# A two-stage transformer block with PEER on one Trainium2 core: the scattered gates are stored in 48 commands of 4 KB rows instead of 12 commands of 16 KB rows

## The chip, the cores and the metric

The kernel runs on 1 core of one Trainium2 chip. Times are device microseconds (us). The kernel before takes 1992.97 us, the median of 3 runs (1991.73 to 1994.1).

## What is computed

One pre-norm layer on 512 tokens of width 1024, all in float32: sliding-window attention and retention side by side, then PEER, then a per-layer embedding gate and a last norm. The change touches PEER alone. For every token and each of 8 heads, PEER takes 16 experts out of 128 x 128 by their scores, and sums them, weighted by a softmax over the 16:

```
top_s, top_pos = lax.top_k(cand, PEER_TOPK)
gates = jax.nn.softmax(top_s, axis=-1)
...
u = jnp.take(expert_down, idx, axis=0)
act = jax.nn.gelu(jnp.einsum('td,ted->te', hx, u, preferred_element_type=jnp.float32))
vv = jnp.take(expert_up, idx, axis=0)
return jnp.einsum('te,ted->td', (act * g).astype(hx.dtype), vv)
```

## The kernel before

**Weights.** All weights pass in 392 units of 128 x 1024 floats (512 KB). SP loads a unit into `raw` (4 slots), ACT rounds it to `w_hi` (L538, function `upper`), POOL subtracts to get `w_lo` (L488, function `lower`), and PE multiplies three times (L923 to L925: high by high, high by low, low by high). SP may load unit u when `lower` of unit u - 4 is done (`lo_done`); `w_hi` and `w_lo` are rings of 8.

**PEER in two ways.** For 384 tokens (12 groups of 32) it is dense: 128 units `dn` give the activations of all experts, 128 units `up` sum them up, and what multiplies the activations is a dense table of gates, zero where an expert was not taken. For the last 128 tokens it is sparse: POOL gathers rows of `peer_down` into 4 slots of `xT` (L512, 512 KB a gather), and DVE makes dot products of them (L1303, `dot`). The table `FETCH_AT` says behind which unit's `lower` POOL issues which gather. POOL works in order: a gather whose slot isn't free yet (`dot_done`) holds up every later `lower` and gather.

**The scatter stage.** Units 64 to 111 of `dn` are six turns (`gate_turn(j)`, j = 0 to 5) of 8 units (c = 0 to 7). In a unit PE makes, beside the 24 matmuls of the unit, two scatters (L1169), each of which spreads the gates of 4 tokens over 128 x 128 experts: one matrix of one-hot rows (DVE, L1659) times one that is multiplied by the gates (DVE L1667 or ACT L768). ACT copies the result from PSUM to `stage` (L755, `stage_gates`). `stage` has two halves, b = 0 and b = 1, each 128 partitions x 128 keys x 32 tokens, 2 MB, one for each half turn (4 units). When one is full, `store_gates` writes it to `gate_scratch` in DRAM (L761); the first copy into the same half, one turn later, waits for `gate_written[b]`. In a unit ACT does, in this order: a `stage_gates`, the products L768, `upper`, the gelu of the unit (L743), after every second one a store of activations to `act_scratch` (L746, 384 KB, rows of 3 KB), the second `stage_gates`, and, at c = 1 and c = 5, `store_gates`. PE may be two scatters ahead of `stage_gates` and two units ahead of the gelu.

**Behind the stage.** After the last turn ACT issues the last store, then makes the high part of `p` (L828), for which DVE waits (L1700) before it goes on with the dots that are left. 16 units of `dn` without scatters follow. The table is read back (L779) from the last eight units on, three key blocks ahead of its use in the `up` stage.

**Queues.** ACT's DMAs all go through one hardware queue (q10 in the profile), SP's through q1, POOL's gathers through q0. In the printed profile names, `stage` is a part of `scr`, so that the store reads `gate_scratch<-scr`.

Of the kernel before, what the change touches and what calls it, by code (L numbers as in the profile page):

```python
# [18 lines left out]
PH, NKEY, TOPK = 8, 128, 16  # L19
# [116 lines left out]
TG = 32  # L136
NTG = TD // TG
# [2 lines left out]
FIRST_Z = 7  # L140
EXP_AT, SELECT_AT = 4, 6
AHEAD = 2
RAW_Q = 4

NPAIR = PH * TOPK
# [31 lines left out]
def row_of(s):  # L177

    if NMAIN <= s < NMAIN + NX:
        return True, s - NMAIN  # L180
    return False, s if s < NMAIN else s - NX
# [15 lines left out]
def block_program(nc, xT_d, w_d, small_d, rope_r_d, decay_d, rope_a_d, mask_d, pT_d, down_d, up_d, out_d):  # L197
# [10 lines left out]
    gate_d = nc.dram_tensor("gate_scratch", (NTG, P, NKEY * TG), F32, kind="Internal").ap()  # L208
# [3 lines left out]
    with ExitStack() as ctx:  # L212
# [3 lines left out]
        def sem(name):  # L216
            return ctx.enter_context(nc.semaphore(name))
# [20 lines left out]
        def cut(at, n):  # L238
            assert at + n <= SCRATCH, (at, n)
            return scr[:, at:at + n]  # L240
# [55 lines left out]
        def v_slot(n):  # L296

            return v_ring[:, n % V_SLOTS, :]
# [9 lines left out]
        stage = cut(0, 8192).rearrange("p (b j t) -> p b j t", b=2, t=TG)  # L308
# [78 lines left out]
        gate_written = [sem("gate_written0"), sem("gate_written1")]  # L387
# [26 lines left out]
        w_rounds = w_d[0:NU // RAW * RAW].rearrange("(r s) p n -> s r p n", s=RAW)  # L414
        gate_quads = gate_d.rearrange("g p (i b n) -> b i p g n", b=2, n=JQ * TG)
        act_quads = act_d.rearrange("(i b a) p n -> b i p a n", b=2, a=2)
        gate_pairs = gate_d.rearrange("(i b) p n -> b i p n", b=2)
        act_pairs = act_d.rearrange("(i a) p n -> a i p n", a=STEP // 2)

        def scattered(q):  # L420
# [43 lines left out]
        @block.sync  # L464
        def _(sp):
            sp.dma_start(raw[:, 0, :], w_d[0]).then_inc(landed[0], 16)
            sp.dma_start(small[:, :], small_d).then_inc(small_landed, 16)
            for i in range(KT // 2):
                sp.dma_start(xT[:, 2 * i:2 * i + 2, :], xT_d[:, 2 * i:2 * i + 2, :]).then_inc(x_landed[i], 16)
            for s in range(1, RAW):  # L470
                sp.dma_start(raw[:, s, :], w_d[s]).then_inc(landed[s], 16)
            with sp.Fori(1, NU // RAW) as r:
                for s in range(RAW):
                    sp.wait_ge(lo_done, RAW * r + (s - RAW + 1))
                    sp.dma_start(raw[:, s, :], w_rounds[s][r]).then_inc(landed[s], 16)
            for u in range(NU // RAW * RAW, NU):
                sp.wait_ge(lo_done, u - RAW + 1)
                sp.dma_start(raw[:, u % RAW, :], w_d[u]).then_inc(landed[u % RAW], 16)
            for k in range(KT):
                sp.wait_ge(final_ready, k + 1)  # L480
                sp.dma_start(out_d[:, k, :], final[:, k, :]).then_inc(stored, 16)
            sp.wait_ge(stored, 16 * KT)


        @block.gpsimd
        def _(pool):
            def lower(s):
                return nc.gpsimd.tensor_tensor(w_lo[:, s, :], raw[:, s % RAW, :], w_hi[:, s, :].bitcast(F32),  # L488
                                               ALU.subtract)

            first = min(FETCH_DOWN) // RING
            with pool.Fori(0, first) as r:
                for s in range(RING):
                    pool.wait_ge(hi_done, RING * r + (s + 1))
                    lower(s).then_inc(lo_done, 1)
            for u in range(first * RING, NU):
                pool.wait_ge(hi_done, u + 1)
                lower(u % RING).then_inc(lo_done, 1)
                for r in FETCH_DOWN.get(u, ()):
                    extra, n = row_of(r)  # L500
                    if r == 0:
                        pool.wait_ge(x_spilled, 16)
                        pool.wait_ge(sq_ready, 2 * KT)
                        pool.wait_ge(h_ready, 3 * KT)
                    if extra:
                        pool.wait_ge(extra_ready, 1)
                    elif n % TOPK == 0:
                        pool.wait_ge(expert_ready, n // TOPK + 1)
                    if r >= U_SLOTS:
                        pool.wait_ge(dot_done, r - U_SLOTS + 1)  # L510
                    ids = expert_extra if extra else expert_of
                    pool.indirect_dma_start(u_ring[:, r % U_SLOTS, :], None, down_d,  # L512
                                            bass.IndirectOffsetOnAxis(ap=ids[:, n:n + 1], axis=0)
                                            ).then_inc(u_landed[r % U_SLOTS], 16)
                for n in FETCH_UP.get(u, ()):
                    if n == 0:
                        for b in range(2):
                            pool.wait_ge(gate_written[b], 16 * (NTG // 2))
                        pool.wait_ge(p_split, 2)
                    if n >= V_SLOTS:  # L520
                        pool.wait_ge(axpy_done, n - V_SLOTS + 1)
                    pool.indirect_dma_start(v_slot(n), None, up_d,  # L522
                                            bass.IndirectOffsetOnAxis(ap=expert_of[:, n:n + 1], axis=0)
                                            ).then_inc(v_landed[n % V_SLOTS], 16)
# [3 lines left out]
        def _(sc):  # L528
# [171 lines left out]
            def key_scores(m):  # L700
                sc.wait_ge(ks_done, m + 1)
                if m >= 8:
                    sc.wait_ge(s12_free, m - 7)
                nc.scalar.activation(s12[:, m % 8].rearrange("p t k -> p (t k)"), bank[:, 2 + m % 2, :],
                                     ACT.Copy).then_inc(s12_ready, 1)
# [3 lines left out]
            for k in range(KT):  # L709
                norm_upper(1, k)  # L710
                if k in (2, 6):
                    m = 1 + (k > 2)
                    run_ahead(UNIT[("pq", m)] + 4)
                    key_scores(m - 1)
            run_ahead(UNIT[("pq", RAW_Q - 1)] + 4)
            key_scores(RAW_Q - 2)
            sc.wait_ge(qp_ready, RAW_Q)
            for m in range(RAW_Q, 2 * PH):
                src = output(("pq", m))
# [29 lines left out]
            def stage_gates(j, q):  # L749

                b, t = q // (TG // 4), 4 * (q % (TG // 4))
                if t == 0 and j > 0:
                    sc.wait_ge(gate_written[b], 16 * j)
                sc.wait_ge(oh_used, 16 * j + (q + 1))
                nc.scalar.activation(stage[:, b, :, t:t + 4], scattered(q).rearrange("p t j -> p j t"),  # L755
                                     ACT.Copy).then_inc(stage_ready, 1)

            def store_gates(j, b):

                sc.wait_ge(stage_ready, 16 * j + 8 * (b + 1))  # L760
                sc.dma_start(gate_pairs[b][j], stage[:, b].rearrange("p j t -> p (j t)")).then_inc(gate_written[b], 16)  # L761

            def gate_odd(j, q):

# [19 lines left out]
            def gate_turn(j):  # L784
                for c in range(STEP):
                    stage_gates(j, 2 * c)
                    if 16 * j + 2 * c + 3 < TD // 4:
                        gate_odd(*divmod(16 * j + 2 * c + 3, 16))
                    gelu(j + (FIRST_Z + 1), c)
                    stage_gates(j, 2 * c + 1)  # L790
                    if c == 1 and j > 0:
                        store_gates(j - 1, 1)
                    if c == 5:
                        store_gates(j, 0)

            sc.wait_ge(filled, 1)
            gelu_turn(0)
# [19 lines left out]
            for j in range(NTG // 2):  # L817
# [3 lines left out]
                if j == TOK_AT[0]:  # L821
                    sc.wait_ge(extra_dotted, 1)
                    nc.scalar.activation(act_extra, turned, ACT.Gelu_apprx_tanh).then_inc(extra_gelu, 1)
            store_gates(NTG // 2 - 1, 1)
            sc.wait_ge(p_landed, 16)
            sc.wait_ge(oh_used, TD // 4)
            for k in range(2):
# [9 lines left out]
            def up_turn(i):  # L837
                last = i == NKEY // STEP - 1
                for c in range(STEP):
                    e = STEP * i + c  # L840
                    upper(UP0 + LEAD + e, (UP0 + LEAD + e) % RING)
                    if not last or c + AHEAD < STEP:
                        weight_upper(e + AHEAD, (c + AHEAD) % STEP)
                    if c % JQ == JQ - 1 and e // JQ + 3 < NKEY // JQ:
# [5 lines left out]
            for c in range(STEP):  # L850
                if c == STEP - 1:
                    for e in range(AHEAD):
                        weight_upper(e, e)
                gelu(NKEY // STEP - 1, c)
                if c == 0:
                    for b in range(2):
                        sc.wait_ge(gate_written[b], 16 * (NTG // 2))
                    read_back(0)
                if c == 3:
                    read_back(1)  # L860
# [59 lines left out]
        def _(pe):  # L920
# [205 lines left out]
            for m in range(2 * PH):  # L1126
                if m < RAW_Q:
                    columns(("pq", m), b_hi, b_lo, tiles=(u_ready, KT) if m == 0 else None,
                            at_tile={KT // 2: lambda: spread(1)} if m == 1 else {})
                else:  # L1130
                    columns(("pq", m), h_hi, h_lo, tiles=(h_ready, 2 * KT) if m == RAW_Q else None)
                if m == RAW_Q:
# [735 lines left out]
```

## Time and profile before

| what | value |
|---|---|
| median of 3 runs | 1992.97 us |
| profiled execution, its own time | 1998.92 us |
| profiled execution, span of the records | 1997.1 us |
| PE busy | 1961.2 us (98%) |
| DVE, POOL, ACT busy | 1313.9, 1226.6, 803.8 us |
| gate stores (L761) | 12 of 2048 KB, median 12.7 us from issue to landing |
| gathers of `peer_down` (L512) | 160 of 512 KB, median 7.0 us |
| weight loads | 390 of 512 KB, median 5.4 us |

The profiled execution took 5.95 us more than the median of the others. The scatter stage lies at about 1060 to 1334 us of the span, the `up` stage at about 1400 to 1900 us. The ends of PE's matmuls are modelled, so its busy time may hold a little of its waiting too.

### The profile page before, as it was taken

To read this page: it belongs to the slowest core of one execution; us is meant where nothing else is said; L and a number is where in the kernel's file an instruction comes from. 1 tells how busy PE (TensorE), PEld (TensorE's weight loads), DVE (VectorE), ACT (ScalarE), POOL (GpSimd) and SP (SyncE) were. 2 spreads that over 40 slices of the span, in tenths; PEclk is the share of its full clock that TensorE was granted. 3 is DMA by queue.
4 is the path that set the end of the run, shared out by engine and by line. 5 is a ranking of instruction groups with operands and counts; after the bars stand their busy time and mean duration, and the time that the engine had idled before them with its cause. 6 is when DMAs were issued, how large, how long until landed. Compare 5 with 4: busy or idle time off the path is not lost.

```text
span 1997.1 us, 28913 instructions
## 1 busy us (share of the span) xinstructions
PE 1961.2 (98%) x10211; PEld 1725.5 (86%) x10211; DVE 1313.9 (66%) x2287; ACT 803.8 (40%) x1273; POOL 1226.6 (61%) x682
## 2 busy tenths in 40 slices
PE   7999999999999999999999999999999999999997
PEld 6888888888888888999999999999888888888886
DVE  6433333333732389988967888861897898888846
ACT  6222222233553333443345666663343333333352
POOL 5342424243234333898877666667899888888821
PEclk9999999999999999999999999999999999999998
DMA  6232313242223332999987999999999999999921
GB/s 210 74 112 62 115 59 107 72 137 80 80 85 95 103 118 79 332 339 329 353 307 258 392 362 365 372 384 315 350 380 387 370 363 355 366 362 363 357 64 43
DMA packets 171953, 471.93 MB, mean 236 GB/s; under 512 B 13776, under 2 KB 62928, under 8 KB 170064
## 3 DMA queue, kind: packets, MB, share of 16 engines
q1 hardware_dynamic: 58032, 209.04, 30.9%
q0 software_dynamic: 41472, 151.01, 19.9%
q10 hardware_dynamic: 72352, 110.64, 15.8%
q8 instruction: 54, 0.88, 0.2%
q14 instruction: 43, 0.35, 0.1%
HBM read 413.49 MB, written 54.53 MB: 234 GB/s over the span
## 4 chain that ended last, share of the span: by engine, by line
PE 69%; DMA 10%; DVE 9%; POOL 8%; issue 2%; ACT 1%; DVEq 0%; SPq 0%; ACTq 0%; POOLq 0%
PE bank L923 22%; PE bank L925 21%; PE bank L924 21%; DMA xT<-peer_down,scr 9%; POOL w_lo L488 6%; POOL xT L512 3%; DVE xT L1303 3%; PE bank L1031 1%; PE bank L1114 1%; DMA gate_scratch<-scr 1%; PE bank L1099 1%; DVE b_hi L1659 1%; DMA raw<-weights 1%; PE bank L1075 0%; PE bank L1085 0%
## 5 line engine op out<-in xcount | busy, mean ns | idle before, releaser
L488 POOL TENSOR_TENSOR w_lo<-raw,w_hi 128x1024 fp32r<-128x1024 f32 x390 | 936.9, 2411 | 570.1 <-ACT w_hi L538 566.0
L923 PE MATMUL bank<-h_hi,w_hi 128*128 128x352 f32 (+2 forms) x1560 | 550.9, 353 | 9.7 <-ACT scr L743 8.9
L925 PE MATMUL bank<-h_hi,w_lo 128*128 128x352 f32 (+2 forms) x1560 | 539.2, 346 | 0.0
L924 PE MATMUL bank<-h_lo,w_hi 128*128 128x352 f32 (+2 forms) x1560 | 538.2, 345 | 0.0
L538 ACT ACTIVATE w_hi<-raw 128x1024 fp32r<-128x1024 f32 x390 | 405.9, 1053 | 283.1 <-DMA raw<-weights 139.4
L923 PEld LDWEIGHTS bank<-h_hi,w_hi 128*128 128x128 f32 x1560 | 294.4, 189 | 31.9 <-POOL w_lo L488 7.3
L924 PEld LDWEIGHTS bank<-h_lo,w_hi 128*128 128x128 f32 x1560 | 295.3, 189 | 19.8
L925 PEld LDWEIGHTS bank<-h_hi,w_lo 128*128 128x128 f32 x1560 | 293.7, 188 | 20.9
L923 PE MATMUL bank<-w_hi,b_hi 128*128 128x512 f32 x768 | 298.8, 389 | 0.0
L925 PE MATMUL bank<-w_hi,b_lo 128*128 128x512 f32 x768 | 298.8, 389 | 0.0
L924 PE MATMUL bank<-w_lo,b_hi 128*128 128x512 f32 x768 | 298.8, 389 | 0.0
L1303 DVE SCALAR_TENSOR_TENSOR xT<-xT,bank 128x1024 f32<-128x1024 f32 x160 | 193.5, 1212 | 78.4 <-DMA xT<-peer_down,scr 74.0
L1732 DVE TENSOR_TENSOR b_lo<-scr,b_hi 128x384 fp32r<-128x384 f32 x128 | 186.6, 1458 | 82.2 <-ACT b_hi L835 81.9
L512 POOL DMA_INDIRECT xT<-peer_down,scr x160 | 151.7, 948 | 122.2 <-DVE xT L1303 88.7
L923 PEld LDWEIGHTS bank<-w_hi,b_hi 128*128 128x128 f32 x768 | 144.1, 188 | 30.0
L925 PEld LDWEIGHTS bank<-w_hi,b_lo 128*128 128x128 f32 x768 | 144.1, 188 | 29.9
L924 PEld LDWEIGHTS bank<-w_lo,b_hi 128*128 128x128 f32 x768 | 144.1, 188 | 29.8
L522 POOL DMA_INDIRECT scr<-peer_up,scr x128 | 137.9, 1077 | 49.0 <-DVE bank L1712 29.0
L835 ACT ACTIVATE b_hi<-scr 128x384 fp32r<-128x384 f32 x128 | 67.2, 525 | 244.0 <-PE bank L925 145.0
L1712 DVE SCALAR_TENSOR_TENSOR bank<-scr,bank 128x1024 f32<-128x1024 f32 x127 | 162.2, 1277 | 0.8
L923 PE MATMUL bank<-b_hi,w_hi 128*128 128x512 f32 x272 | 108.1, 398 | 10.5 <-DVE b_lo L1318 9.1
L923 PE MATMUL bank<-w_hi,h_hi 128*128 128x512 f32 (+1 forms) x288 | 109.7, 381 | 1.1 <-DVE h_lo L1351 1.1
(215 smaller groups left out, 2446.9 us busy)
## 6 DMA issues: line engine op xcount, KB each, us to landing
raw<-weights SPq DMA_DIRECT2D x390, 512.0 KB, 5.4
act_scratch<-scr ACTq DMA_DIRECT2D x64, 384.0 KB, 5.8
gate_scratch<-scr ACTq DMA_DIRECT2D x12, 2048.0 KB, 12.7
scr<-gate_scratch ACTq DMA_DIRECT2D x22, 768.0 KB, 9.9
scr<-act_scratch ACTq DMA_DIRECT2D x22, 768.0 KB, 15.4
xT<-gate_scratch ACTq DMA_DIRECT2D x10, 768.0 KB, 9.1
xT<-act_scratch ACTq DMA_DIRECT2D x10, 768.0 KB, 13.8
scr<-scr ACTq DMA_DIRECT2D x20, 128.0 KB, 2.9
```

Source lines behind the costliest of these rows:

```text
L488: return nc.gpsimd.tensor_tensor(w_lo[:, s, :], raw[:, s % RAW, :], w_hi[:, s, :].bitcast(F32), ALU.subtract)
L512: pool.indirect_dma_start(u_ring[:, r % U_SLOTS, :], None, down_d, bass.IndirectOffsetOnAxis(ap=ids[:, n:n + 1], axis=0)).then_inc(u_lande ...
L522: pool.indirect_dma_start(v_slot(n), None, up_d, bass.IndirectOffsetOnAxis(ap=expert_of[:, n:n + 1], axis=0)).then_inc(v_landed[n % V_SLOT ...
L538: nc.scalar.activation(w_hi[:, u_mod, :], raw[:, s, :], ACT.Copy).then_inc(hi_done, 1)
L835: nc.scalar.activation(b_hi[:, c % 4, 0:TD], wgt[:, c % 2, :], ACT.Copy).then_inc(wgt_hi_ready, 1)
L923: nc.tensor.matmul(out, a_hi, c_hi, start=first, stop=False)
L924: nc.tensor.matmul(out, a_hi, c_lo, start=False, stop=False)
L925: return nc.tensor.matmul(out, a_lo, c_hi, start=False, stop=last)
L1031: ins = nc.tensor.matmul(bank[:, 2 + j, 0:S - P * j], r_k[:, c, P * j:P * j + P], r_q[:, c, P * j:S], start=c == 0, stop=c == 1)
L1303: stt(out=row, in0=row, scalar=1.0, in1=h_tok, op0=ALU.mult, op1=ALU.mult, accum_out=to[:, n:n + 1]).then_inc(dot_done, 1)
L1712: ins = stt(out=y_sparse, in0=v_slot(n), scalar=a, in1=y_sparse, op0=ALU.mult, op1=ALU.add)
L1732: tt(b_lo[:, c % 4, 0:TD], wgt[:, c % 2, :], b_hi[:, c % 4, 0:TD].bitcast(F32), ALU.subtract).then_inc(wgt_split, 1)
```

## The change

A half of `stage` is written by four commands instead of one, each for 32 of the 128 keys: 128 partitions x 1024 floats, 4 KB in a row at both ends, 512 KB a command. Two are issued one unit earlier than the one command was, behind c = 4 (or c = 0), and two where it was, behind c = 5 (or c = 1). The last half has its four commands together. The waits count 4 x 16 for a half. The bytes and their places in DRAM stay, and so does everything that reads them.

```
+GATE_PARTS = 4
...
-        gate_pairs = gate_d.rearrange("(i b) p n -> b i p n", b=2)
+        gate_parts = gate_d.rearrange("(i b) p (j t) -> b i p j t", b=2, t=TG)
...
                 if t == 0 and j > 0:
-                    sc.wait_ge(gate_written[b], 16 * j)
+                    sc.wait_ge(gate_written[b], 16 * GATE_PARTS * j)
...
-            def store_gates(j, b):
+            def store_gates(j, b, parts):
 
                 sc.wait_ge(stage_ready, 16 * j + 8 * (b + 1))
-                sc.dma_start(gate_pairs[b][j], stage[:, b].rearrange("p j t -> p (j t)")).then_inc(gate_written[b], 16)
+                for x in parts:
+                    part = slice(x * NKEY // GATE_PARTS, (x + 1) * NKEY // GATE_PARTS)
+                    sc.dma_start(gate_parts[b][j][:, part], stage[:, b, part, :]).then_inc(gate_written[b], 16)
...
-                    if c == 1 and j > 0:
-                        store_gates(j - 1, 1)
-                    if c == 5:
-                        store_gates(j, 0)
+                    if c in (0, 1) and j > 0:
+                        store_gates(j - 1, 1, (2 * c, 2 * c + 1))
+                    if c in (4, 5):
+                        store_gates(j, 0, (2 * c - 8, 2 * c - 7))
...
-            store_gates(NTG // 2 - 1, 1)
+            store_gates(NTG // 2 - 1, 1, range(GATE_PARTS))
```

ACT's instructions at units c = 4 and c = 5 of the first turn, where the first half is stored; `scr<-bank` of L755 are the copies into `stage`. Before:

```order
L755 ACTIVATE scr<-bank 128x128x4 x2
L768 ACTIVATE scr<-b_hi,scr 128x128 x4
L538 ACTIVATE w_hi<-raw 128x1024
L743 ACTIVATE scr<-bank 128x352
L746 DMA act_scratch<-scr 128x768
L755 ACTIVATE scr<-bank 128x128x4
L761 DMA gate_scratch<-scr 128x4096
L755 ACTIVATE scr<-bank 128x128x4
```

The same place of the changed kernel (its lines stand one to three lower):

```order
L756 ACTIVATE scr<-bank 128x128x4
L764 DMA gate_scratch<-scr 128x1024 x2
L756 ACTIVATE scr<-bank 128x128x4
L771 ACTIVATE scr<-b_hi,scr 128x128 x4
L539 ACTIVATE w_hi<-raw 128x1024
L744 ACTIVATE scr<-bank 128x352
L747 DMA act_scratch<-scr 128x768
L756 ACTIVATE scr<-bank 128x128x4
L764 DMA gate_scratch<-scr 128x1024 x2
```

The first two parts now stand ahead of a store of activations in ACT's queue, the other two behind it. ACT behind the last turn, before:

```order
L746 DMA act_scratch<-scr 128x768
L755 ACTIVATE scr<-bank 128x128x4
L761 DMA gate_scratch<-scr 128x4096
L828 ACTIVATE b_hi<-scr 128x512 x2
L538 ACTIVATE w_hi<-raw 128x1024
```

and in the changed kernel:

```order
L747 DMA act_scratch<-scr 128x768
L756 ACTIVATE scr<-bank 128x128x4
L764 DMA gate_scratch<-scr 128x1024 x4
L831 ACTIVATE b_hi<-scr 128x512 x2
L539 ACTIVATE w_hi<-raw 128x1024
```

Four commands now stand ahead of the high part of `p` where there was one.

## Rows read from the trace of the kernel before

**Rows 1.** Busy time by stretch: stretch, length, engines (us, count), PEclk, DMA share, GB/s.

```profile
1058.30:1061.70 3.40, 3.40 (x15) 3.40 (x15) 1.93 (x4) 1.52 (x5) 3.22 (x3) 0.50 0.79 235
1069.50:1336.50 267.00, 266.57 (x1897) 265.63 (x1896) 214.18 (x284) 169.58 (x371) 184.40 (x121) 1.00 0.94 357
1336.50:1372.00 35.50, 33.09 (x205) 32.54 (x204) 11.88 (x20) 12.79 (x18) 25.83 (x14) 1.00 0.91 332
1400.00:1900.00 500.00, 500.00 (x2207) 414.01 (x2207) 430.34 (x376) 188.93 (x249) 439.87 (x254) 1.00 1.00 365
```

**Rows 2.** PE in order of time: start, duration, instruction, [idle before <- releaser].

```profile
1057.39 0.40 PE L923 MATMUL bank<-h_hi,w_hi 128*128 128x352 f32 x1 [3.54 <-ACT scr L743]
...
1158.95 1.16 PE L1169 MATMUL bank<-scr,b_lo 128*128 128x128 f32 x8 [0.37 <-DVE scr L1667]
...
1353.94 0.43 PE L923 MATMUL bank<-h_hi,w_hi 128*128 128x352 f32 x1 [0.52 <-POOL w_lo L488]
...
1359.96 0.40 PE L923 MATMUL bank<-h_hi,w_hi 128*128 128x352 f32 x1 [1.89 <-ACT scr L743]
```

**Rows 3.** The chain of waits ahead of PE's last two restarts: start, us, what.

```profile
1329.87 19.14 DMA xT<-peer_down,scr
...
1349.03 1.24 DVE xT L1303 x2
...
1351.48 2.40 POOL w_lo L488
...
1357.59 2.23 DMA raw<-weights
```

**Rows 4.** DVE in order of time, ahead of the restart at 1158.95.

```profile
1155.94 1.22 DVE L1303 SCALAR_TENSOR_TENSOR xT<-xT,bank 128x1024 f32<-128x1024 f32 x1 [4.43 <-DMA xT<-peer_down,scr]
```

**Rows 5.** DMA queues from 1341 to 1346: packets, MB, share of 16 engines.

```profile
DMA packets 203, 2.15 MB, mean 429 GB/s; under 512 B 21, under 2 KB 21, under 8 KB 89
...
q10 hardware_dynamic: 119, 1.87, 87.4%
q0 software_dynamic: 79, 0.26, 12.8%
```

**Rows 6.** DMA queues from 1337 to 1340.

```profile
DMA packets 341, 1.22 MB, mean 406 GB/s; under 512 B 18, under 2 KB 18, under 8 KB 341
...
q1 hardware_dynamic: 119, 0.48, 40.8%
q0 software_dynamic: 119, 0.42, 36.1%
q10 hardware_dynamic: 103, 0.31, 25.8%
```

**Rows 7.** DMA queues from 1346 to 1351: the gathers'.

```profile
q0 software_dynamic: 275, 1.01, 49.4%
```

**Rows 8.** ACT in order of time: two gelus, two gate stores.

```profile
1100.23 0.45 ACT L743 ACTIVATE scr<-bank 128x352 f32<-128x352 f32 x1
...
1105.86 0.44 ACT L743 ACTIVATE scr<-bank 128x352 f32<-128x352 f32 x1
...
1324.99 0.71 ACTq L761 DMA_DIRECT2D gate_scratch<-scr  x1
...
1334.89 0.33 ACTq L761 DMA_DIRECT2D gate_scratch<-scr  x1
```

**Rows 9.** Who waited for whom, 1066 to 1330: us in total, times, longest.

```profile
ACT scr L755 <- PE bank L1169: 44.2, 31, 3.9
...
ACT scr L755 <- DMA gate_scratch<-scr: 10.4, 4, 3.7
```

**Rows 10.** DVE and POOL behind the last gate store.

```profile
1342.93 1.22 DVE L1303 SCALAR_TENSOR_TENSOR xT<-xT,bank 128x1024 f32<-128x1024 f32 x1 [3.05 <-DMA xT<-peer_down,scr]
...
1339.30 0.95 POOL L512 DMA_INDIRECT xT<-peer_down,scr  x1 [6.09 <-DVE xT L1303]
```

**Rows 11.** The gathers of `peer_down` (L512) issued from 1095 to 1335.

```profile
DMA to landing us min/median/max: 4.3/11.0/19.1
```

More of the change, by code:

```diff
@@ L517, in _ @@
                         for b in range(2):
-                            pool.wait_ge(gate_written[b], 16 * (NTG // 2))
+                            pool.wait_ge(gate_written[b], 16 * GATE_PARTS * (NTG // 2))
                         pool.wait_ge(p_split, 2)
@@ L856, in _ @@
                     for b in range(2):
-                        sc.wait_ge(gate_written[b], 16 * (NTG // 2))
+                        sc.wait_ge(gate_written[b], 16 * GATE_PARTS * (NTG // 2))
                     read_back(0)
```

## The prediction, made before the changed kernel ran

> **What bounds the kernel now.** The page shows PE busy for 98% of the span, so a store in another engine's queue can only matter where PE waits. Where that is, the stretches say [rows 1]. From the first gate store to the end of the scatter stage (1069.5 to 1336.5) PE is busy for 266.57 of 267.00 us; in the 35.5 us behind it for 33.09. So all that PE loses where a gate store is in flight is 0.43 + 2.41 = 2.84 us. Ahead of 1069.5 the change does nothing, and the `up` stage (1400 to 1900) has PE at 500.00 of 500.00 us although its DMA share is 1.00.
>
> PE in order of time shows the same loss as three restarts [rows 2]: idle for 0.37 us at 1158.95, 0.52 at 1353.94 and 1.89 at 1359.96, together 2.78 us.
>
> What do they hang on? The chain of waits answers for the last two [rows 3]: a gather of `peer_down` issued at 1329.87 lands after 19.14 us, the dot at 1349.03 waits for it, POOL's next gather waits for the dot's slot, `lower` at 1351.48 stands behind that gather, and PE waits for this `lower` at 1353.94. The weights that came late through all this land last (1357.59), and make the wait of 1.89 us. The restart at 1158.95 waits for DVE's L1667, which stands behind a dot that waited 4.43 us for its gather [rows 4]. So all three hang on gathers that land late, none on ACT's own wait for a gate store. Those waits are there (4, together 10.4 us, the longest 3.7) but ACT has cover for them: it waits 44.2 us for PE in the same stretch [rows 9].
>
> Why do the gathers land late? The DMA queues from 1341 to 1346 [rows 5]: 203 packets, of which only 89 are under 8 KB; the other 114 are the 16 KB rows of the last gate store. Its queue has 87.4% of the engines and the gathers 12.8%, though a gather is pending all the time. Four us earlier, where q10 still moves activations in rows of 3 KB, the three queues have 40.8, 36.1 and 25.8% [rows 6]. **A queue gets its turn by packets, not by bytes: rows of 16 KB push the others aside, rows of 3 or 4 KB share.**
>
> **The change part by part.**
>
> *Rows of 4 KB instead of 16 KB.* This is the part with a gain. In the 5 us of [rows 5] the gathers moved 0.26 MB. With the share of [rows 6] it is 0.42 MB in 3 us, so 0.70 MB in 5 us: 0.44 MB more by 1346. Behind that the gathers ran at 1.01 MB in 5 us, 0.20 MB per us [rows 7], so the late one lands 0.44 / 0.20 = 2.2 us earlier. The whole chain of [rows 3] hangs on it and moves by 2.2 us. To do away with both restarts it would have to move by 0.52 + 1.89 = 2.41 us. Gain 2.2, and 0.2 stays. The restart at 1158.95 is 0.37 us behind a wait of 4.43 for a gather, and goes: gain 0.4. Bounds: nothing (the gather is late for another reason) to 2.84 (every stall goes).
>
> *Four commands instead of one.* 36 commands more on ACT. A command took 0.33 to 0.71 us [rows 8]. In a scatter turn they are two more at c = 0 and c = 4, at most 1.4 us in a unit's 5.63 us (the distance of two gelus, the same rows), and one more at c = 1 and c = 5, at most 0.7. ACT waits for PE 31 times, 44.2 us in all [rows 9], 1.4 us each, just behind the `stage_gates` where the commands now stand. Price 0; with that cover gone, 1.4 us per half turn.
>
> The Trainium skill, "DMA: Bandwidth & Descriptors", section "Rules for kernel authors", speaks against this part: at least 1 MiB per DMA. Its section "Anatomy of one DMA" has, for the path through GpSimd, a fit of 2.0 us fixed plus the bytes at 436 GB/s for each. By that, as an estimate, four commands of 512 KB would need 6 us more than one of 2 MB if nothing overlapped. The trace doesn't bear it out for queued commands: the weights and gathers of [rows 6] are commands of 512 KB, and the engines moved 406 GB/s beside 429 for the large rows of [rows 5].
>
> That ratio is the price in engine time: 2 MB take 5.2 us of all engines instead of 4.9, 0.3 us for each of 12 halves, 3 us in a stretch with a DMA share of 0.94 over 267 us, so 16 us free [rows 1]. Hidden.
>
> *Half of it a unit earlier.* The store now shares, so it takes longer, and it has 16.9 us (three units of 5.63) from its first command to the copy that needs the half, instead of 11.3. Suppose q10 has only the even share all the time: 2.1 MB at 0.16 MB per us (0.48 MB in 3 us for rows of 4 KB, [rows 6]) are 13.1 us, 0.39 MB of activations between them at 0.10 are 3.8, and I allow 2 for a command's start (the last store, issued at 1334.89, ran from about 1341 on behind activations). That is 18.9 us, 2.0 more than there is. ACT then waits 2 us per half, in the range of what it now waits (up to 3.7) without a restart of PE. With the others idle at times the share is higher and there is no wait. Price 0.
>
> *The last half, four commands ahead of L828.* Three more commands delay `p`'s high part by 3 x 0.33 = 1.0 to 3 x 0.71 = 2.1 us. Behind it: DVE's L1700, the dots, and POOL, which waited 6.09 us for a dot [rows 10]. The dot at 1342.93 waits 3.05 us for its gather anyway, which takes up the delay on DVE; the gathers POOL issues at 1339.30 are later by as much, and are used only behind 1350. Price 0; bounds 0 and 2.1.
>
> **Sum.** 2.2 + 0.4 = 2.6 us off. On the profiled execution 1998.92 becomes 1996.3; on the median, 1992.97 becomes **1990.4 us**. The medians lie 5.95 us under the profiled time; what the profiler adds is not known, and if it adds DMA work, the unprofiled runs may have less of these stalls to lose.
>
> 0.2% is 4.0 us, about what a measurement of this kernel can tell from no change. So even the whole 2.84 us would count as no change.
>
> **Rivals.**
>
> *The gathers don't profit (chance 0.20).* Sharing may go by commands, or the last gather may be late for what stands ahead of it in its own queue (19.14 us is more than the 5 us of one gate store). For it: two gate stores, of 1324.99 and 1334.89, fall into its flight, and one command can hold only part of that. Against it: the even shares of [rows 6] with rows of 3 and 4 KB. Then 1992 to 1994, no change.
>
> *More than 4.0 us (0.11).* The stalls that show are worth 2.84. PE's busy time is modelled and may hold waits of a few hundredths at many of the scatters; for 94 half units in 267 us, 0.015 us each would be 1.4, together 4.2 us: 1988.8. Faster.
>
> *ACT becomes late (0.07).* The other side. The place is the first copy into a half of `stage`. From the first command it has 16.9 us and some 3.7 us of wait that PE didn't feel, 20.6 us. If q10 gets less than its even share, say 0.12 MB per us, a half takes 2.1 / 0.12 + 3.8 + 2 = 23.3 us, and PE waits 2.7 us in each of ten half turns (the first and the last have no successor): 1992.97 + 27 - 0.4, about 2020 us. It decides from a landing of the second pair some 15 us behind its issue.
>
> *The end gets worse (0.05).* The 2.1 us of the last four commands go through to PE, nothing is won, and the wait of 1.89 us becomes 4.0. A wait of 3.54 us at 1057.39 [rows 2] was followed by 3.4 us in which the granted clock was 0.50, 1.2 GHz [rows 1], 1.7 us lost. Together 3.8 to 4.5 us: 1997.
>
> **How the numbers follow.** The forecast has 0.57, the rivals 0.20, 0.11, 0.07 and 0.05. Faster 0.11, same 0.77, slower 0.12. The range: down to 1992.97 - 2.84 - 1.2 (the spread of the runs shown) - 0.5 (a third of the hidden waits) = 1988.4, with some 0.08 of the fast case under it; up to 1992.97 + 2.5 = 1995.5, where the rival without a gain pays the upper bound of 2.1 for the last four commands, with the two slow cases over it.
>
> **What would show it.** Right: queue q10 has at most half of the engines while gates are stored; the median landing of L512 from 1095 to 1335 falls under its 11.0 us [rows 11]; the three restarts are gone or one of under 1 us is left behind 1350; ACT's wait for `gate_scratch` is no longer than 4 us; PE busy for over 34.5 of the 35.5 us behind the stage. Wrong: gathers still at 11 us or more with rows of 4 KB in q10 (sharing is not by packet), or PE idle in the scatter stage with ACT L755 behind `gate_scratch` (the store is too slow).

## The result, and the profile after

The changed kernel takes 1998.43 us, median of 20 runs (1993.44 to 2007.28), beside 1991.93 us for the kernel before (20 runs, 1987.88 to 1995.4): a ratio of 1.0029, 95% interval 1.002 to 1.0037. It is slower, by 5.8 us by this ratio and by 6.5 us from median to median, where 2.6 us less was forecast, and outside the range. (Of the weights, the section on the kernel speaks of 392 units; the profile's loads are 390.)

The profiled execution of the changed kernel took 1995.74 us, 3.2 us less than the profiled one before. That pair misleads: 1998.92 us was more than every one of the 20 runs before, and 1995.74 is the sixth fastest of the 20 after.

Stretches of the changed kernel, as [rows 1]:

```profile
1069.50:1336.50 267.00, 267.00 (x1902) 267.00 (x1901) 214.95 (x282) 168.28 (x372) 183.09 (x120) 1.00 0.97 369
1336.50:1372.00 35.50, 32.22 (x202) 31.95 (x201) 10.89 (x19) 12.96 (x19) 28.98 (x16) 1.00 0.85 280
```

PE is never idle in the scatter stage, but loses 3.28 us behind it, where it lost 2.41. Who waited for whom there, from 1066 to 1330, as [rows 9]:

```profile
POOL xT L513 <- DVE xT L1306: 44.3, 30, 3.4
...
ACT scr L756 <- DMA gate_scratch<-scr: 13.5, 4, 4.9
...
DVE xT L1306 <- DMA xT<-peer_down,scr: 5.2, 4, 2.9
```

The gathers do land earlier, issued from 1095 to 1335, as [rows 11]:

```profile
DMA to landing us min/median/max: 4.9/8.1/12.1
```

So the half of the prediction that spoke of the gathers came true: the median fell from 11.0 to 8.1 us, DVE's wait for them from 34.7 (20.8 in the second trace of the kernel before) to 5.2 us, and the restart at 1158.95 is gone. What came instead stands behind the last turn. ACT in order of time (ACTq marks the commands that ACT issues):

```profile
1330.46 0.60 ACT L756 ACTIVATE scr<-bank 128x512 f32<-128x512 f32 x1 [0.43 <-PE bank L1172]
1331.09 3.24 ACTq L764 DMA_DIRECT2D gate_scratch<-scr  x4
1334.44 1.16 ACT L831 ACTIVATE b_hi<-scr 128x512 fp32r<-128x512 f32 x2 [3.37 <-issue]
```

DVE and POOL at the same place, as [rows 10]:

```profile
1335.17 1.42 DVE L1703 TENSOR_TENSOR b_lo<-scr,b_hi 128x512 fp32r<-128x512 f32 x2 [11.86 <-ACT b_hi L831]
...
1338.41 0.95 POOL L513 DMA_INDIRECT xT<-peer_down,scr  x1 [11.22 <-DVE xT L1306]
```

The chain of waits from there to PE, in order of time, as [rows 3]:

```profile
1331.09 0.33 ACTq L764
1331.45 0.54 ACTq L764
1332.01 1.05 ACTq L764
1333.10 1.24 ACTq L764
1334.44 0.64 ACT b_hi L831
...
1336.62 1.24 DVE xT L1306 x2
...
1348.95 2.42 POOL w_lo L489
1351.53 4.85 DMA raw<-weights
```

and PE's restart at its end:

```profile
1356.75 0.40 PE L926 MATMUL bank<-h_hi,w_hi 128*128 128x352 f32 x1 [3.29 <-ACT scr L744]
```

**The four commands of the last half hold ACT for 3.24 us, each longer than the one ahead of it.** The high part of `p` waits behind them, DVE waits for `p` with its last dots behind that, POOL waits for the dots with its gathers and `lower`s, and these free the slots of the weights.

The second trace of the kernel before (below), in which PE loses nothing here, shows the same three places:

```profile
1329.72 0.33 ACTq L761 DMA_DIRECT2D gate_scratch<-scr  x1
...
1330.89 1.42 DVE L1700 TENSOR_TENSOR b_lo<-scr,b_hi 128x512 fp32r<-128x512 f32 x2 [8.95 <-ACT b_hi L828]
...
1334.13 0.95 POOL L512 DMA_INDIRECT xT<-peer_down,scr  x1 [8.31 <-DVE xT L1303]
```

The store holds ACT for 0.33 us there and for 3.24 us in the changed kernel, 2.91 us more. DVE's wait for `p` is longer by 2.91 us too, and POOL's wait for the dots by 2.91 us. PE loses 3.28 us at the end of this chain.

In 9 of the 20 runs the mean granted clock was 0.996 or more, with a mean time of 1996.0 us; in 11 it was 0.995 or less, with a mean of 2000.5.

### The profile page after: what moved, and what is told of

The parts are those of the page before. It is cut to its first block, busy times and chain, and to the rows that moved or that the text cites. A ratio compares the mean times of both kernels' runs of the same rounds, so it can differ in the third digit from the quotient of the medians.

```text
span 1993.9 us, 28949 instructions
## 1 busy us (share of the span) xinstructions
PE 1957.6 (98%) x10211; PEld 1724.2 (86%) x10211; DVE 1310.4 (66%) x2287; ACT 802.3 (40%) x1273; POOL 1227.2 (62%) x682
## 4 chain that ended last, share of the span: by engine, by line
PE 81%; POOL 7%; DVE 6%; DMA 3%; ACT 1%; issue 1%; ACTq 0%; DVEq 0%; SPq 0%; POOLq 0%
PE bank L926 24%; PE bank L928 24%; PE bank L927 24%; POOL w_lo L489 5%; PE bank L1172 4%; POOL xT L513 2%; DMA xT<-peer_down,scr 2%; DVE xT L1306 1%; PE bank L1034 1%; DMA raw<-weights 1%; PE bank L1117 1%; PE bank L1102 1%; PE bank L1078 0%; PE bank L1088 0%; DVE scr L1597 0%
```

## The experiments

Two theories. **E, the end**: the loss is the hold of ACT ahead of `p`, behind the last turn. **S, the stage**: the store, sharing the engines, comes late for the copies into `stage`, half turn for half turn.

### The changed kernel again; `p` first; the last half in one command

Four kernels: the changed one again (`a_again`); the changed one with the high part of `p` ahead of the last store (`a_pfirst`); the kernel before with the same move (`b_pfirst`); the changed one with its last half stored in one command, as before (`a_lastone`).

```
# a_pfirst, b_pfirst: moved ahead of the last store_gates
sc.wait_ge(p_landed, 16)
sc.wait_ge(oh_used, TD // 4)
for k in range(2):
    nc.scalar.activation(b_hi[:, 6 + k, :], pT[:, k, :], ACT.Copy).then_inc(p_hi_ready, 1)
# a_lastone: the last half
sc.dma_start(gate_last, stage[:, 1].rearrange("p j t -> p (j t)")).then_inc(gate_written[1], 16)
```

Changed kernel again. 

> The changed kernel once more, as the measure for its neighbours on the same chip. Theory E (the end): its loss comes from behind the last scatter turn, where four commands hold ACT for about 3 us ahead of the high part of p, and PE idles 3 to 4 us near 1353; the time is then 4 to 7 us over the kernel before, and the trace shows no stall of PE from 1095 to 1335. Theory S (the stage): the loss is made of waits of the copies into the stage for their store, and the trace shows PE stalls there.

`p` first, changed kernel. 

> The changed kernel with the high part of p ahead of the last half's four commands instead of behind them. Theory E: the delay of DVE behind the last turn shrinks by some 3 us, PE's stall near 1353 by 3 us, and the time falls by 3 to 6 us against the changed kernel, to the kernel before or under it. Theory S: no change against the changed kernel, 5 to 6 us over the kernel before.

`p` first, kernel before. 

> The kernel before with the same move. Its one command took 0.33 us there. Theory E: at most 0.5 us less than before, so no difference. If it gains more than 2 us, what matters is not ACT's time for the command but that p is ready earlier for another reason.

Last half in one command. 

> The changed kernel with the last half stored by one command of 2 MB in rows of 16 KB, as before; the other eleven halves stay in four commands each. Theory E: the time falls to that of the kernel before (within 2 us), since ACT is held for 0.3 instead of 3.2 us. Theory S: no change against the changed kernel. If the last store's rows of 16 KB push the gathers and weights aside (the prediction's mechanism), this one is slower than the variant with p ahead by 1 to 2 us.

| kernel | median us (runs) | ratio to before, 95% |
|---|---|---|
| before, same chip | 1993.34 (35) | |
| changed, again | 1998.05 (12) | 1.0025 (1.0012 to 1.0038) |
| changed, `p` first | 1991.8 (12) | 0.9994 (0.9981 to 1.0006) |
| before, `p` first | 1992.1 (12) | 0.9996 (0.998 to 1.0011) |
| changed, last half in one | 1991.68 (12) | 0.9994 (0.9981 to 1.0008) |

Each of the two, `p` first and the last half in one command, takes the whole loss of the changed kernel away, 6.3 and 6.4 us from median to median, with 11 halves still in four commands and their rows of 4 KB. So E holds, and S falls. On the kernel before, `p` first makes no difference that can be told, as expected. That the rows of 16 KB of the last store cost 1 to 2 us more than four commands behind `p` does not show.

The second trace of the changed kernel has what the first lacked. Its four commands:

```profile
1332.36 3.27 ACTq L764 DMA_DIRECT2D gate_scratch<-scr  x4
```

PE's restart, two matmuls behind it and two some microseconds later:

```profile
1358.77 0.63 PE L926 MATMUL bank<-h_hi,w_hi 128*128 128x352 f32 x1 [4.04 <-ACT scr L744]
...
1363.60 0.49 PE L927 MATMUL bank<-h_lo,w_hi 128*128 128x352 f32 x1
1363.90 0.49 PE L928 MATMUL bank<-h_hi,w_lo 128*128 128x352 f32 x1
...
1364.65 0.32 PE L928 MATMUL bank<-h_hi,w_lo 128*128 128x352 f32 x1
1364.81 0.33 PE L926 MATMUL bank<-h_hi,w_hi 128*128 128x352 f32 x1
```

The stretches there:

```profile
1357.70:1364.40 6.70, 5.63 (x19) 5.66 (x20) 1.13 (x2) 3.29 (x5) 6.05 (x3) 0.50 0.86 264
...
1336.50:1372.00 35.50, 31.46 (x180) 31.20 (x180) 12.13 (x20) 12.71 (x18) 26.61 (x15) 0.90 0.79 261
```

The granted clock is 0.50 (1.2 GHz) for 6.7 us, from the last 1.07 us of an idle time of 4.04 us on. The 18 matmuls from 1358.77 to 1364.19 take 5.4 us, about 0.29 us from start to start; at the 0.16 us of the rows behind them they would take 2.9. So the clock costs some 2.5 us on top of the wait. The span is 2000.0 us, as against 1993.9 in the first trace, where 3.29 us of idle were followed by no such stretch. Of the 6.1 us, 2.5 are the clock and 0.75 the longer wait; 1.3 lie ahead of the last store (1332.36 as against 1331.09), and PE loses 1.1 us in the `up` stage (498.91 busy of 500.00). With `p` first:

```profile
1336.50:1372.00 35.50, 35.50 (x224) 35.50 (x223) 6.06 (x10) 14.11 (x20) 30.30 (x15) 1.00 0.95 316
```

PE has no idle time left here and the clock stays at 1.00; the span is 1988.6 us. ACT is held no less than before, but now with `p` ahead of it:

```profile
1329.26 0.86 ACTq L764 DMA_DIRECT2D gate_scratch<-scr  x2
...
1330.14 2.63 ACTq L764 DMA_DIRECT2D gate_scratch<-scr  x2
...
1333.09 0.95 POOL L513 DMA_INDIRECT xT<-peer_down,scr  x1 [7.72 <-DVE xT L1306]
```

`upper` and the gelus stand behind these commands as well, and nothing is lost.

### The end alone; the dots first; one command with small rows; the kernel before again

```
# b_lastfour: kernel before, the last half alone (gate_last = gate_d[NTG - 1]; the waits count 48 more)
for x in range(4):
    sc.dma_start(gate_last[:, 1024 * x:1024 * x + 1024],
                 stage[:, 1, 32 * x:32 * x + 32].rearrange("p j t -> p (j t)")).then_inc(gate_written[1], 16)
# a_dotsfirst: changed kernel, on DVE
next_dots(NLAST)                      # was behind the split of p
ve.wait_ge(oh_used, TD // 4)
for k in range(2):
    ve.wait_ge(p_hi_ready, k + 1)
    ...
# b_rows4k: DRAM laid out (NTG, P, 4, 1024 + 128), one command per half
sc.dma_start(gate_rows[b][j], stage[:, b].rearrange("p (x j) t -> p x (j t)", x=4))
```

The end alone. 

> The kernel before with the last half alone in four commands of 4 KB rows; the other eleven halves as before. Theory E (four commands back to back hold ACT for some 3.2 us ahead of the high part of p): the whole loss is here, 4 to 7 us over the kernel before, PE idle for 3 to 4.5 us near 1353, and in some runs a stretch at 1.2 GHz behind it. Rival (the end only hurts because the earlier gathers of the changed kernel bring DVE to its wait for p sooner): under 2 us over the kernel before.

Dots first. 

> The changed kernel with the last dots of DVE ahead of its wait for p instead of behind it; ACT keeps its order. Theory E says that the late p costs only because the dots, and with them POOL's gathers and lower parts, stand behind it on DVE: the time falls by 4 to 7 us against the changed kernel, POOL's wait of 11 us behind the last turn goes, and PE has no stall near 1353. Rival (ACT's delay of 3 us itself reaches PE, through the weights' high part or the gelu): no change against the changed kernel.

Rows of 4 KB in one command. 

> The kernel before with its one command per half, at its place, but in rows of 4 KB (four parts of a row lie 512 B apart in DRAM): the size of the rows alone. By the prediction's mechanism the gathers land in 8 to 9 us instead of 11 in the scatter stage, and PE has no stall there; the time is that of the kernel before less 0 to 3 us, and ACT issues the command in under 1 us. If rows of 4 KB cost ACT as much as four commands do, the issue of the last one takes about 3 us and the time is 4 to 7 us over the kernel before.

The kernel before again. 

> The kernel before once more, for a second trace. Its first trace took 1998.9 us, more than any unprofiled run near it. If the stalls of PE behind the last turn (2.4 us in the first trace) are typical, they are here again; if they were bad luck, PE is never idle from 1095 to 1900 and the span is near 1990 us, so that the changed kernel had nothing to win.

| kernel | median us (runs) | ratio to before, 95% |
|---|---|---|
| before, same chip | 1991.55 (19) | |
| before, last half in four | 1995.98 (10) | 1.0023 (1.0012 to 1.0033) |
| changed, dots first | 1990.55 (10) | 0.9997 (0.9986 to 1.0009) |
| before, one command, rows of 4 KB | 2013.62 (4) | 1.0116 (1.0094 to 1.0137) |
| before, again | 1992.35 (1) | |

Splitting **the last half alone** costs 4.4 us from median to median, where the changed kernel lost 6.5 and, in its repetition, 4.7. The intervals of the ratios overlap, so no rest is shown. PE restarts at 1354.63:

```profile
1354.63 0.40 PE L927 MATMUL bank<-h_hi,w_hi 128*128 128x352 f32 x1 [3.57 <-ACT scr L744]
```

followed by 3.2 us at a granted clock of 0.50:

```profile
1356.10:1359.30 3.20, 3.20 (x13) 3.20 (x12) 0.00 (x0) 1.33 (x2) 3.20 (x3) 0.50 0.76 247
```

With **the dots first**, ACT is still held,

```profile
1332.05 2.09 ACTq L764 DMA_DIRECT2D gate_scratch<-scr  x4
```

yet PE's busy time behind the stage is full and the loss is gone:

```profile
1336.50:1372.00 35.50, 35.50 (x224) 35.50 (x223) 7.55 (x12) 14.52 (x20) 24.87 (x12) 1.00 0.89 317
```

So ACT's hold reaches PE through DVE, where the dots stand behind `p`, and not through ACT's own work. The hold is also shorter here, 2.09 us; why, these runs don't tell, and by itself this trace would leave open that the shorter hold made the difference. `p` first doesn't: there ACT was held for 2.63 us by the last two commands alone.

**The kernel before**, in its second trace:

```profile
1069.50:1336.50 267.00, 267.00 (x1900) 267.00 (x1899) 217.88 (x288) 169.56 (x370) 184.07 (x123) 1.00 0.96 367
1336.50:1372.00 35.50, 35.50 (x224) 35.50 (x223) 6.64 (x12) 14.05 (x20) 31.27 (x15) 1.00 0.92 326
```

None of the 2.84 us of [rows 1] is there, so in this execution the change had nothing to win. Of the 6.5 us between the two spans (1997.1 and 1990.6), 5.2 lie ahead of the last gate store (issued at 1334.89 and at 1329.72). The expectation failed in one point: PE does lose 1.17 us in the `up` stage (498.83 busy of 500.00).

**Rows of 4 KB in one command** cost 22 us, where a gain of 0 to 3 was expected. The gathers do land somewhat earlier (a median of 8.9 us over 1095 to 1336.5, as against 9.3 in the second trace of the kernel before), but the other side of sharing decides: the store lands late. Landings of the gate stores, and the waits from 1095 to 1336.5:

```profile
DMA to landing us min/median/max: 13.9/16.9/20.5
```

```profile
ACT scr L758 <- DMA gate_scratch<-scr: 57.9, 10, 8.8
...
PE bank L1172 <- ACT scr L758: 11.0, 5, 3.1
```

The median landing of the store was 12.7 us in the first trace before and 11.5 in the second. Now it is late for 10 half turns and PE idles for 11.0 us; what makes up the rest of the 22 I did not part. ACT issues the command in 0.52 us, so small rows by themselves don't hold ACT.

### All four at the old place; four commands of 16 KB rows; both moves

```
# a_notearly: all four where the one was
if c == 1 and j > 0:
    store_gates(j - 1, 1, range(GATE_PARTS))
if c == 5:
    store_gates(j, 0, range(GATE_PARTS))
# b_cmds4: kernel before, four commands of 32 partitions, rows of 16 KB
for x in range(4):
    at = slice(32 * x, 32 * x + 32)
    sc.dma_start(gate_pairs[b][j][at], stage[at, b].rearrange("p j t -> p (j t)")).then_inc(gate_written[b], 16)
```

None early. 

> The changed kernel with all four commands of a half where the one command was, none a unit earlier. The one command with 4 KB rows at that place landed after 16.9 us, over the 11.3 us that are left, ACT waited 57.9 us and PE was late by 11 us in the stage, 22 us in all. If the share of q10 makes that (rows of 4 KB share, whoever issues them), this kernel too is 15 to 30 us slower than before, with PE waiting for the copies into the stage. If it was the single command or its padded rows in DRAM, this one is at the changed kernel, 4 to 7 us over before.

Four commands, large rows. 

> The kernel before with every half in four commands of 32 partitions each, rows of 16 KB, at the place of the one: the count of commands alone. Theory E: ACT is held for about 3 us ahead of the high part of p, and the loss is that of the last four commands alone, 3 to 6 us; in the stage no stall of PE. If the rows' size makes ACT's hold, there is none here (0.33 us a command) and the time is that of before. If four commands per half hold ACT inside the stage too, over 8 us.

Both moves (`p` first and dots first), changed kernel. 

> The changed kernel with both mends, the high part of p ahead of the last store and the last dots ahead of the wait for p. Each alone took away the stall near 1353, so together they should give no more: within 2 us of either, 0 to 3 us under the kernel before, not to be told from it. If the earlier gathers of the 4 KB rows are worth something once the end is mended, it shows here as more than 2 us under the same two moves on the kernel before.

Both moves, kernel before. 

> The kernel before with the same two moves. PE had no stall from 1095 to 1900 in its second trace, so 0 to 2 us under the kernel before.

| kernel | median us (runs) | ratio to before, 95% |
|---|---|---|
| before, same chip | 1993.07 (29) | |
| changed, none early | 2003.87 (10) | 1.0045 (1.003 to 1.006) |
| before, 4 x 32 partitions | 2016.38 (4) | 1.0114 (1.009 to 1.0138) |
| changed, both moves | 1992.1 (12) | 0.9998 (0.9985 to 1.0012) |
| before, both moves | 1991.27 (12) | 0.9992 (0.998 to 1.0004) |

Without the unit's lead the changed kernel loses 10.8 us from median to median (9.0 by the ratio), some 3 to 4 more than with it (6.5 and 5.8), and under the 15 to 30 expected. The intervals of the two ratios overlap a little (1.003 to 1.006, and 1.002 to 1.0037); what tells the two apart is the trace. The store is late again, less than in `b_rows4k`, where ACT waited 57.9 us for it. Waits of ACT from 1095 to 1336.5:

```profile
ACT scr L756 <- DMA gate_scratch<-scr: 40.1, 9, 6.8
ACT scr L756 <- issue: 25.4, 7, 5.6
```

PE waits 4.6 us for these copies, where it waited for none in the changed kernel. "Issue" is ACT held by its own commands, which now are four in a row in every half turn.

Four commands of 32 partitions with rows of 16 KB fit only the third reading of their expectation. ACT is held inside the stage too:

```profile
ACT scr L755 <- issue: 38.0, 8, 6.0
ACT scr L755 <- DMA gate_scratch<-scr: 27.1, 10, 4.4
```

The longest row of four held ACT for 6.50 us. So four commands in a row hold ACT with rows of 16 KB too. This kernel also keeps the late gathers, and I did not part its 23 us further.

The two moves together give no more than each alone, and on neither kernel a difference from the kernel before that can be told. No version here beats the kernel before.

## Why the prediction was wrong

- **The baseline was the first error.** "So all that PE loses where a gate store is in flight is ... 2.84 us": true of that execution, which took 5.95 us more than the median. I named that gap, asked only what the profiler might add, and still took the stalls of that one execution for those of the kernel. The second trace has none; in it the term of 2.6 us is worth 0, and the medians of the two kernels with both moves (1992.1 changed, 1991.27 before) show no gain either. Besides, the first gate store is issued at 1095.5, not at 1069.5 as the prediction says; for the sum that makes no difference, as the stalls lie behind both. And the weights of [rows 3] start at 1357.59 and take 2.23 us; they land at 1359.82.
- **The step that failed: "The last half, four commands ahead of L828 ... Price 0; bounds 0 and 2.1".** Three more commands were sized at 0.33 to 0.71 us from single commands. In a row they took 0.54, 1.05 and 1.24, 2.8 us together. And the cover was wrongly read. The wait of 3.05 us for a gather [rows 10] is one that DVE has at 1342.93; the gather that POOL issues at 1339.30 waits for an earlier dot, and behind that gather stand POOL's `lower`s, which free the slots of the weights. On that path nothing took up the delay: POOL waited 8.31 us in the second trace before without a loss for PE, and 11.22 us in the changed kernel with 3.28 us lost. The price of this term, measured alone, is 4.4 us.
- **The rival "The end gets worse" (0.05) is what happened**, by its mechanism: 3.8 to 4.5 us estimated, 5.8 measured. The clock takes part in two of the three traces that show this loss, with 3.2 and 6.7 us at 1.2 GHz; in the first trace of the changed kernel it doesn't. Its price was put at half of the slow stretch, 1.7 of 3.4 us; by the distances of the matmuls (0.29 us in place of 0.16) it is nearer 1.5. A chance of 0.05 for a row of four commands ahead of a barrier was too small.
- **Packets, not bytes: right in the main.** Gathers from 11.0 to 8.1 us, against 9.3 in the second trace before (in a median over 1095 to 1336.5), so that part of the 2.9 us belongs to the first execution. But the sign "q10 has at most half of the engines" was wrong: from 1186 to 1191 it had 67.6%, with rows of 4 KB. The gathers' queue used 7.1% then: POOL issued one gather at 1180.16 and the next at 1191.54, so this stretch shows the sign failing and not an uneven sharing.
- **"Half of it a unit earlier", price 0: right.** ACT waited for the store 4 times, 13.5 us in all, beside an estimate of 2 us in each half turn, and PE, busy for 267.00 of 267.00 us, did not feel it. The longest wait, 4.9 us, is over the 4 us that were set as the limit. The mechanism of the rival "ACT becomes late" showed itself where that lead is missing, with landings of 16.9 us at a point set to "some 15 us behind its issue".
- **The Trainium skill's rule** ("DMA: Bandwidth & Descriptors", section "Rules for kernel authors") asks for at least 1 MiB per DMA for the highest bandwidth. The change did come out slower, but not through bandwidth: in the stretch of [rows 1] from 1069.5 the engines moved 369 GB/s, as against 357 and 367 in the two traces before. What the runs show as the price is the issuing engine's time.

## What to carry to other kernels

Ask of a split command not only what it does to the queues, but what stands behind it on the engine that issues it: put what others wait for ahead of a row of commands. Where a kernel has a barrier at the end of a stage, follow its queue on every engine; the engine without cover was two steps away. And take a second trace of the baseline ahead of any sum over its stalls, above all where the profiled execution is slower than all the others.

## What the runs showed of the hardware

- Commands of 128 rows of 4 KB, issued in a row on ACT's queue behind the last turn, took ACT 0.33, 0.54, 1.05 and 1.24 us; four took 2.09 to 3.27 us there, and up to 6.13 us inside the stage (`a_notearly`). Four of 32 rows of 16 KB took up to 6.50 us. One command of 512 rows of 4 KB took 0.52 us. Why commands in a row take longer is not shown.
- Rows of 16 KB in one queue left another queue with a gather pending 12.8% of the engines [rows 5]; with rows of 4 KB the gathers' median landing was 8.1 us, as against 11.0 and 9.3 in the two traces before, and a store of 2 MB in one command landed in 16.9 us instead of 12.7 and 11.5.
- Idle times of PE of 3.54, 3.57 and 4.04 us were followed by 3.4, 3.2 and 6.7 us at a granted clock of 0.50; one of 3.29 us in the changed kernel was not, while one of 1.97 us in the second trace of the kernel before (at 1053.54, ahead of the stores) was. So the length of the idle time alone does not decide it. In the case of 4.04 us the low clock began 1.07 us before the restart.
